# Cached values as the stationary operand in the sample attention of a hybrid attention layer

## The reference

```
def _band_attn_sample(q, k_new, v_new, k_cache, v_cache, rel_bias):
    ...
    sc = jnp.einsum('bqhd,bkhd->bhqk', q, k).astype(jnp.float32) * (d ** -0.5)
    sc = sc + _rel_bias(rel_bias, dist)[None]
    p = jax.nn.softmax(sc, axis=-1).astype(v.dtype)
    o = jnp.einsum('bhqk,bkhd->bqhd', p, v)
    return o.reshape(b, n, h * d)
```

## Time and profile before

| | us |
|---|---|
| timed runs, median of 3 | 2840.66 |
| lowest and highest | 2838.58, 2840.94 |
| the profiled execution | 2838.89 |
| span in its profile | 2837.1 |
| TensorE busy in the span | 2599.5 (92%) |
| TensorE weight loads busy | 2322.3 (82%) |
| VectorE busy | 1368.5 (48%) |
| ScalarE busy | 993.4 (35%) |

### The profile page before, as it was taken

How to read it: one execution, slowest core, us unless ns; L and a number is a source line. 1 busy time by engine, 2 the same in 40 slices (tenths; PEclk the granted TensorE clock), 3 DMA queues, 4 the chain that set the end, 5 groups by cost and what they waited for, 6 DMA issues and landing times. The chain is left out here.

```text
span 2837.1 us, 39977 instructions
## 1 busy us (share of the span) xinstructions
PE 2599.5 (92%) x16468; PEld 2322.3 (82%) x16468; DVE 1368.5 (48%) x2391; ACT 993.4 (35%) x1691; POOL 606.9 (21%) x448
## 2 busy tenths in 40 slices
PE   3899999999998999976988989989589999999997
PEld 2899999978878799975776766658489999998886
DVE  6333323244554598985767723332723233234544
ACT  5333333334332313133666532221433333323432
POOL 6333334300001022831000000000344433320000
PEclk9999999999999999987999989999799999999999
DMA  3112222266632121213000334551022121226553
GB/s 104 47 62 79 69 87 79 68 235 219 214 137 67 47 95 64 81 49 121 23 30 24 119 106 151 180 195 52 32 75 79 62 79 62 93 85 243 202 206 126
DMA packets 153108, 294.27 MB, mean 104 GB/s; under 512 B 14032, under 2 KB 90456, under 8 KB 152928
## 3 DMA queue, kind: packets, MB, share of 16 engines
q1 hardware_dynamic: 146688, 268.12, 27.9%
q0 software_dynamic: 6240, 23.59, 2.3%
HBM read 237.26 MB, written 61.78 MB: 105 GB/s over the span
## 5 line engine op out<-in xcount | busy, mean ns | idle before, releaser
L786 DVE TENSOR_TENSOR f_dl<-f_raw_d,f_dh 128x2048 fp32r<-128x2048 f32 x66 | 151.3, 2293 | 274.8 <-ACT f_dh L573 274.8
L573 ACT ACTIVATE f_dh<-f_raw_d 128x2048 fp32r<-128x2048 f32 x66 | 126.5, 1916 | 322.4 <-PE f_pV L151 292.1
L149 PE MATMUL f_pX<-f_xop,f_g_shi 128*128 128x256 f32 (+1 forms) x528 | 159.8, 303 | 18.8 <-ACT f_gh L523 18.8
L523 ACT ACTIVATE f_gh<-f_pX 128x256 f32<-128x256 f32 (+1 forms) x132 | 54.2, 410 | 335.7 <-PE f_pX L151 335.6
L2062 PEld LDWEIGHTS t_po<-t_v,t_pT 128*128 128x128 f32 x1056 | 135.1, 194 | 34.0 <-DVE t_osb L1786 14.3
L149 PE MATMUL f_pX<-f_xop,f_u_shi 128*128 128x256 f32 (+1 forms) x528 | 157.2, 298 | 4.4 <-ACT f_tu L523 4.4
L150 PE MATMUL f_pX<-f_xop,f_g_shi 128*128 128x256 f32 (+1 forms) x528 | 158.7, 301 | 0.0
L151 PE MATMUL f_pX<-f_xop,f_g_slo 128*128 128x256 f32 (+1 forms) x528 | 158.7, 300 | 0.0
L1919 ACT ACTIVATE t_sc<-t_sc,t_small 128x640 f32<-128x640 f32 (+8 forms) x136 | 100.0, 735 | 164.0 <-DVE t_small L1847 129.8
L150 PE MATMUL f_pX<-f_xop,f_u_shi 128*128 128x256 f32 (+1 forms) x528 | 156.8, 297 | 0.0
L151 PE MATMUL f_pX<-f_xop,f_u_slo 128*128 128x256 f32 (+1 forms) x528 | 156.8, 297 | 0.0
(11 more groups left out here) (333 smaller groups left out, 8100.0 us busy)
## 6 DMA issues: line engine op xcount, KB each, us to landing
f_raw_d<-in_ffn_w_down SPq DMA_DIRECT2D x66, 1024.0 KB, 4.9
hid<-f_gh SPq DMA_DIRECT2D x22, 1152.0 KB, 8.6
f_raw_h<-hid SPq DMA_DIRECT2D x66, 384.0 KB, 5.5
f_g_raw<-in_ffn_w_gate SPq DMA_DIRECT2D x22, 1024.0 KB, 5.4
f_u_raw<-in_ffn_w_up SPq DMA_DIRECT2D x22, 1024.0 KB, 6.4
proj<-w_stage POOLq DMA_DIRECT2D x12, 1152.0 KB, 5.6
i_raw<-in_w_in SPq DMA_DIRECT2D x12, 1024.0 KB, 5.2
f_x<-in_x_prompt SPq DMA_DIRECT2D x16, 512.0 KB, 6.4
```

The lines of the kernel that those rows point to most:

```text
L149: pe.matmul(out, a[0], b[0], start=first, stop=False, skip_group_check=goes_on)
L523: act.activation(dst, by_tile(pX[:, c, 0:N[c]]), ACT.Copy).then_inc(s_copy, 1)
L573: act.activation(d_hi[slot(q)][:], raw_d[slot(q)][:], ACT.Copy).then_inc(s_dhi, 1)
L786: dve.tensor_tensor(d_lo[slot(q)][:], raw_d[slot(q)][:], d_hi[slot(q)][:].bitcast(F32), ALU.subtract)
```

## The change

In the value step the operands change places. The stationary operand is now a block of the cached values for a pair of heads (128 keys x 128, two heads of 64), the moving one the 32 columns of `pT` that hold these two heads' queries. There are four pairs, so each item has 4 x 5 matmuls in place of 5, and the result comes out in turned form: 128 partitions are (head of the pair, value), columns are (pair, head, query). It lies in `po` for even items and in `pm` for odd ones. The transposes of the out step and `osb` are no longer used; ScalarE and VectorE read each head's own block (`own_block`) straight from `po` or `pm`. Since a row sum now belongs to a column, VectorE scales the exponentials before they are turned: at the end of the score step it waits for ScalarE's exponential, takes the reciprocal and scales the 128 x 528 tile in place.

```diff
+        def own_block(s, r):
+
+            a = (po, pm)[s % 2][r * HD:(r + 1) * HD, 0:P]
+            return a.rearrange("p (f c) -> p f c", c=2 * DEC_S)[:, :, r * DEC_S:(r + 1) * DEC_S]
...
                     dve.tensor_scalar(small[:, 1, g % 4:g % 4 + 1], small[:, 0, g % 4:g % 4 + 1], -1.0, None, ALU.mult).then_inc(s_sc, 1)
+                    dve.wait_ge(s_p, g + 1)
+                    dve.reciprocal(rec[:, n % 2, 0:1], sums[:, 0, s % H:s % H + 1]).then_inc(s_rc, 1)
+                    dve.wait_ge(s_rc, n + 1)
+                    dve.tensor_scalar(sc_of(g, 0, KS), sc_of(g, 0, KS), rec[:, n % 2, 0:1], None, ALU.mult).then_inc(s_nm, 1)
...
-                elif e == "value":
-                    dve.wait_ge(s_o, g + 1)
-                    dve.reciprocal(rec[:, n % 2, 0:1], sums[:, 0, s % H:s % H + 1]).then_inc(s_rc, 1)
-                    dve.wait_ge(s_rc, n + 1)
-                    if s >= 2:
-                        dve.wait_ge(s_mf, misc[("so", s - 2)] + 1)
-                    dve.tensor_scalar(osb[:, n % 2, :], po[:], rec[:, n % 2, 0:1], None, ALU.mult).then_inc(s_os, 1)
...
                 elif e == "out":
-                    act.wait_ge(s_mf, misc[("so", s)] + 1)
+                    act.wait_ge(s_o, g + 1)
...
-                        i = act.activation(oT_hi[r * HD:(r + 1) * HD, x * HT:(x + 1) * HT, cs], diag(r), ACT.Copy)
+                        i = act.activation(oT_hi[r * HD:(r + 1) * HD, x * HT:(x + 1) * HT, cs], own_block(s, r), ACT.Copy)
...
                 elif e == "turn":
-                    pe.wait_ge(s_p, g + 1)
+                    pe.wait_ge(s_nm, s + 1)
...
                 elif e == "value":
-                    pe.wait_ge(s_os, NTT + s)
+                    if s >= 2:
+                        pe.wait_ge(s_ma, misc[("so", s - 2)] + 1)
+                        pe.wait_ge(s_ml, lo_n[("so", s - 2)])
+                    elif s:
+                        pe.wait_ge(s_ma, misc[("so", 0)])
+                    else:
+                        pe.wait_ge(s_os, NTT)
...
-                    for k in range(PAST // P):
-                        pe.matmul(po[:], pT[:, s % 2, k * P:(k + 1) * P], vc[s % 2][:, k, :], start=k == 0, stop=False)
-                    pe.matmul(po[:], pT[0:DEC_S, s % 2, PAST:PAST + P], vn[s % 2][:], start=False, stop=True).then_inc(s_o, 1)
-                else:
-                    pe.wait_ge(s_os, NTT + s + 1)
-                    pe_rows(pe, ("so", s), osb[:, (NTT + s) % 2, :])
+                    out, w = (po, pm)[s % 2], 2 * DEC_S
+                    for f in range(HT):
+                        fs = slice(f * P, (f + 1) * P)
+                        for k in range(PAST // P):
+                            pe.matmul(out[:, f * w:(f + 1) * w], vc[s % 2][:, k, fs], pT[:, s % 2, k * P + f * w:k * P + (f + 1) * w],
+                                      start=k == 0, stop=False)
+                        last = pe.matmul(out[:, f * w:(f + 1) * w], vn[s % 2][:, fs], pT[0:DEC_S, s % 2, PAST + f * w:PAST + (f + 1) * w],
+                                         start=False, stop=True)
+                    last.then_inc(s_o, 1)
```

More of the change, by code:

```diff
@@ L1601, in attn_phase @@
         s_sr = sem("sample_rows_loaded")
+        s_nm = sem("sample_probabilities_scaled")
         heads, plan = attn_plan()
@@ L1772, in _ @@
                     pool.wait_ge(s_bd, 3 * s + j + 1)
-        def diag(r):
-            a = pm[r * HD:(r + 1) * HD, 0:DEC_S]
-            return bass.AP(a.tensor, a.offset + r * DEC_S, [list(a.ap[0]), [P + 2 * DEC_S, HT], [1, DEC_S]])
+        def own_block(s, r):
+            a = (po, pm)[s % 2][r * HD:(r + 1) * HD, 0:P]
+            return a.rearrange("p (f c) -> p f c", c=2 * DEC_S)[:, :, r * DEC_S:(r + 1) * DEC_S]
         def dve_out(dve, key, n):
@@ L1899, in _ @@
                                 dve.tensor_copy(pT[0:DEC_S, s % 2, PAST:PAST + P], pt[u % 2][0:DEC_S, 0:P]).then_inc(s_pt[1], 1)
-                elif e == "value":
-                    dve.wait_ge(s_o, g + 1)
-                    dve.reciprocal(rec[:, n % 2, 0:1], sums[:, 0, s % H:s % H + 1]).then_inc(s_rc, 1)
-                    dve.wait_ge(s_rc, n + 1)
-                    if s >= 2:
-                        dve.wait_ge(s_mf, misc[("so", s - 2)] + 1)
-                    dve.tensor_scalar(osb[:, n % 2, :], po[:], rec[:, n % 2, 0:1], None, ALU.mult).then_inc(s_os, 1)
-                else:
+                elif e == "out":
                     m = misc[("so", s)]
@@ L1912, in _ @@
                     for r in range(2):
-                        i = dve.tensor_tensor(oT_lo[r * HD:(r + 1) * HD, fs, cs], diag(r),
+                        i = dve.tensor_tensor(oT_lo[r * HD:(r + 1) * HD, fs, cs], own_block(s, r),
                                               oT_hi[r * HD:(r + 1) * HD, fs, cs].bitcast(F32), ALU.subtract)
```

## The result

The changed kernel takes 2879.5 us (median of 4 runs, 2876.5 to 2881.6) against 2840.8 before: a ratio of 1.0132, with an interval of 1.0115 to 1.0150. It is slower, and within 1.5 us of the predicted 2881. The profiled execution has a span of 2879.9 us, 42.8 more than before.

The account below looks back on a forecast made before the run. TensorE's own sequence was taken to set the pace in the sample attention. 2838.89 + 8.3 at full clock + 33 for the clock gave 2880 us profiled, 2881 median; range 2862 to 2903, 8 in 10 over all cases 2842 to 2900.

Parts of the forecast that it names:

- The value step: TensorE's value matmuls per item: 5.27 us against 4.58 at full clock, +0.69 us per item.
- eight changes: Switches between 128-row and 16-row stationary operands in each value step, four pairs: 0.90 us per item.
- The output transposes and the scaling: Four transposes per item removed, 0.44 us, and VectorE's scaling moved into the score step: both 0 in the loop.
- the case that the cover is gone: If key copies no longer hid the four output transposes, removing them would save 0.44 us per item.
- The beginning: First turning of the sample attention: TensorE waits longer for reciprocal and scaling, +1.0 us (0.6 to 1.8).
- The clock: TensorE's clock falls to 1.2 GHz in nearly every sample attention item and the last two value steps: +33 us.
- rival 1: The clock holds because TensorE never stands still in the new step; only +8.3 us, median 2849 us; chance 0.16.
- 13 x 1.7 = 22: Loop's clock loss in us: one 3.4 us low stretch per item at about half speed, over 13 items.
- The end: Stage's end after the loop: -1.7 us at full clock, but 10.6 us lost with the last two value steps low.
- Rivals 2 and 3: Free height changes: clock falls in every other item, median 2855 us, chance 0.13; or clock holds, 2835 us, chance 0.07.
- The forecast's own range: Total time if the clock falls and height changes are paid: 2862 to 2903 us.
- the +8.3 of the full clock: Sample attention's loop, beginning and end without clock loss: 9.0 + 1.0 - 1.7 = +8.3 us.

Follow-up runs that it names:

- the padded kernel: The changed kernel, still 32 columns per matmul, with the 16 new values zero-padded to 128 rows: 2857.8 us, ratio 1.0056.
- padded 128-column kernel: The changed kernel with all 128 columns of pT per value matmul and new values zero-padded to 128 rows: 2838.8 us, ratio 0.9987 to the kernel before.
- the first of the interleaved ones: Changed kernel with 128 columns, zero-padded new values and key transposes moved between value matmuls, transfer order unaltered: 2861.8 us, ratio 1.0060 to the kernel before.

## Why the prediction was right

**The value step.** Predicted 5.27 us at full clock, measured 5.26. Its two parts stand apart in the padded kernel: without changes of height 4.38 (predicted 4.37), so that eight changes cost 0.88 (0.90). The cadence of loads taken from other stages held for 32 columns: (0.97 - 0.19)/7 = 0.111 us.

**The output transposes and the scaling.** Nothing in the loop, as predicted; the runs with one transpose and with the scaling alone both kept the 11.74 us item. The -0.44 per item that the prediction names for the case that the cover is gone was 0.49 when it was.

**The beginning.** Right in direction, mis-sized. The scaling took 0.49 us, not the 0.75 of its nearest row, and the wait grew by 0.72, not 1.0; but the clock, which stayed at 1.00 behind the wait of 1.86, fell behind the wait of 2.58, and the stretch cost 2.8, some 2.1 of it by the clock. The padded 128-column kernel, which loses the clock nowhere else in the stage, pays the same 2.8 there (6.91 and 10.25 against 6.19 and 8.15). A wait was priced by its length only. But its length doesn't decide by itself: of the nine kernels with this wait of 2.58 us, eight had the low stretch right behind it, and the first of the interleaved ones did not.

```profile
1701.14 0.77 PE L2006 MATMUL t_pt<-r_ident,t_sc 128*128 128x128 f32 x5 [2.58 <-DVE t_sc L1899]
...
1697.50:1709.50 12.00, 7.76 (x45) 6.07 (x44) 4.08 (x13) 3.33 (x7) 1.40 (x6) 1.00 0.45 165
```

Of the five with the wait of 1.86, four kept 1.00 through the first turnings, and the one with a single output transpose lost it some 8 us later. What else decides stays open.

**The clock.** It fell in each of the 13 items, as forecast, and rival 1 (it holds because TensorE never stands still) is out: TensorE was busy 156.67 of 160 us at 0.82, and 152.62 at 1.00 with 128 columns. The rule of the Trainium skill that stood behind this rival ("TensorE: Matmul & The Clock Gate", Why this matters for your kernels: no idle gaps between bursts) doesn't cover this kernel, whose clock fell in the middle of a step without a gap. The size, 13 x 1.7 = 22, came out nearly right by luck, from two misses that cancel. There was one low stretch per item, as forecast, but a longer one: 72 us in all, 5.5 per item, where 3.4 were assumed. The longest are three times that:

```profile
1712.80:1722.90 10.10, 10.10 (x43) 8.71 (x43) 1.66 (x3) 1.79 (x3) 0.00 (x0) 0.50 0.40 131
```

And each cost less than half its length: 34.1 - 9.0 = 25.1 us over 72, 0.35 for each low microsecond and not 0.5. Part of the loss falls into time in which TensorE waits anyway at full clock: 16 key transposes at the lower level take 1736.45 - 1732.76 = 3.69 us, where the same step at full clock, with its waits for the copies out of pt, takes 2.72 in the padded 128-column kernel, +0.97 instead of a doubling of the 16 x 0.11 of matmul time.

**The end.** +7.0 against +8.9: the last two value steps ran low nearly throughout, as predicted, but took 9.5 and 9.6 us and not 10.6 each, since a group of ten matmuls takes 2.41 us at the lower level and 1.34 at the higher, 1.8 times and not twice.

The evidence for the fall was weaker than the prediction has it. The low stretch that it blames on few columns per load began at 1670 us, while TensorE stood waiting for a transfer:

```profile
1672.90 0.85 PE L2071 MATMUL t_ps<-t_raw_s,t_flip_s 128*128 128x144 f32 x2 [3.17 <-DMA t_raw_s<-urel]
```

And 64 columns, the width of the matmuls before it, kept the clock in the items at one height. That 32 columns would lose it was shown by the runs, not by that row.

Rivals 2 and 3 needed free changes of height; at 0.11 us a change they were not. The forecast's own range has a slip: its lower end of 2862 leaves out the +8.3 of the full clock, and with it every other item gives 2870; nothing else rests on it.

What stays open: why 64 columns with bare loads lose the clock and 64 without don't. Six points of columns and heights don't separate the time between matmuls from the columns in them.

## What to carry to other kernels

Count the moved columns per loaded operand before operands change places: the exchange saved four transposes that cost nothing, and paid with 40 loads in place of 10 and with the clock. Whether work that is removed was on the path is decided by what stands beside it; here a copy out of a PSUM buffer had to go first, and then the same exchange, with wide matmuls and one height, was part of the fastest version (2820 us). And when a step moves forward in one engine's order, its transfers have to move forward in their queue.

## What the runs showed of the hardware that was not expected

At a change of the stationary operand's height between 128 and 16 rows the columns of the matmul before are bare: a pair of changes cost 0.22 us at 32 columns (0.88 over four) and 0.36 at 128 (1.44 over four), and padding the 16 rows to 128 with zeros made the kernel before faster by 0.25%. TensorE's clock fell to 1.2 GHz inside steps without any gap, at 32 columns per load in every item of the changed kernel, and at 64 columns where loads stood bare or value steps followed each other. And behind a wait of 2.58 us it stood at 1.2 GHz for 3.4 us in eight of nine kernels, and right behind one of 1.86 us in none of five; the clock then cost some 2.1 us, three times the 0.72 by which the wait had grown.
